# Retention decay factors: exponents built on VectorE in place of ScalarE's scale and bias

## The reference

```python
def retention_chunked(q, k, v, s0, log_gamma):
    diff = pos[:, None] - pos[None, :]
    decay = jnp.exp(jnp.where(diff >= 0, diff * lg, -jnp.inf))
...
        scores = jnp.einsum('bhid,bhjd->bhij', qc, kc) * decay
        o = jnp.einsum('bhij,bhje->bhie', scores, vc) + jnp.einsum('bhid,bhde->bhie', qc * q_dec, s)
...
def bidir_prefix(scan_f, scan_b, lat_f, lat_b, ctx_f, ctx_b):
    o_cf, s_f = scan_f(*ctx_f, s0)
    o_cb, s_b = scan_b(*flip(ctx_b), s0)
    o_lf, _ = scan_f(*lat_f, s_f)
    o_lb, _ = scan_b(*flip(lat_b), s_b)
    return o_lf + o_lb[:, :, ::-1], o_cf + o_cb[:, :, ::-1]
```

## Time and profile before

| | |
|---|---|
| median of 3 runs | 2225.99 us (2222.12 to 2227.66) |
| the profiled execution | 2222.12 us, span 2220.3 us |
| mean granted TensorE clock | 0.952 |
| PE / DVE / ACT / POOL busy | 92% / 43% / 34% / 33% of the span |
| the retention stage | from 811 to 891 us of the span |

### The profile page before, as it was taken

One profiled execution on the slowest core, in us unless ns is written; L12 is line 12 of the kernel. 1 busy time (PEld: TensorE's weight loads), 2 busy tenths in 40 slices (PEclk: granted clock), 3 DMA queues, 4 the chain that ended last, 5 costly groups with the idle time before them and its releaser, 6 DMA issues.

```text
span 2220.3 us, 26492 instructions
## 1 busy us (share of the span) xinstructions
PE 2039.9 (92%) x9550; PEld 1691.7 (76%) x9550; DVE 944.2 (43%) x1397; ACT 749.8 (34%) x1051; POOL 732.3 (33%) x324
## 2 busy tenths in 40 slices
PE   5999999999899989689899999979588888999997
PEld 2999999999868764556788888757464756888886
DVE  5652476145436026973411111377836535121124
ACT  4221122112263144342432222445446343232331
POOL 0323233323224220332344443523330222543432
PEclk9999999999999999678999999989789998999999
DMA  7432344334222210001233232322130211322321
GB/s 310 133 113 76 114 142 145 101 114 146 71 67 77 66 55 20 10 1 57 76 101 107 91 101 92 113 67 76 53 113 8 68 58 57 114 90 91 114 81 61
DMA packets 53273, 197.19 MB, mean 89 GB/s; under 512 B 6304, under 2 KB 6864, under 8 KB 51408
## 3 DMA queue, kind: packets, MB, share of 16 engines
q1 hardware_dynamic: 44272, 162.98, 23.0%
q10 hardware_dynamic: 8928, 33.23, 4.3%
HBM read 194.09 MB, written 2.10 MB: 88 GB/s over the span
## 4 chain that ended last, share of the span: by engine, by line
PE 78%; issue 9%; DVE 6%; ACT 3%; POOL 2%; DMA 1%; SPq 0%; DVEq 0%; POOLq 0%; ACTq 0%; PEldq 0%
PE ps L1606 64%; PE ps L1620 2%; POOL wlo L497 2%; PE ps L1593 1%; PE ps L1594 1%; PE ps L1595 1%; PE ps L1864 1%; DMA ada_f<-ada_p 1%; PE ps L1799 1%; PE ps L1925 1%; PE ps L1792 1%; PE ps L1951 1%; DVE prod L1083 1%; DVE s_gla L1347 1%; PE ps L1840 1%
## 5 line engine op out<-in xcount | busy, mean ns | idle before, releaser
L497 POOL TENSOR_TENSOR wlo<-raw,whi 128x1024 fp32r<-128x1024 f32 x280 | 690.8, 2479 | 1370.8 <-ACT whi L533 1348.7
L1606 PE MATMUL ps<-h_hi,whi 128*128 128x512 f32 (+2 forms) x1584 | 515.4, 364 | 13.8 <-POOL wlo L497 6.6
L1606 PE MATMUL ps<-h_hi,wlo 128*128 128x512 f32 (+2 forms) x1584 | 512.8, 362 | 0.0
L1606 PE MATMUL ps<-h_lo,whi 128*128 128x512 f32 (+2 forms) x1584 | 512.4, 362 | 0.0
L533 ACT ACTIVATE whi<-raw 128x1024 fp32r<-128x1024 f32 x280 | 289.6, 1053 | 425.6 <-PE ps L1606 342.1
L1606 PEld LDWEIGHTS ps<-h_hi,whi 128*128 128x128 f32 x1584 | 290.4, 188 | 56.6 <-issue 10.8
L1606 PEld LDWEIGHTS ps<-h_lo,whi 128*128 128x128 f32 x1584 | 290.3, 189 | 33.6 <-issue 0.7
L1606 PEld LDWEIGHTS ps<-h_hi,wlo 128*128 128x128 f32 x1584 | 290.1, 188 | 33.5
L1606 PE MATMUL ps<-g_hi,wlo 128*128 128x512 f32 (+1 forms) x784 | 257.4, 364 | 0.0
L1606 PE MATMUL ps<-g_hi,whi 128*128 128x512 f32 (+1 forms) x784 | 257.4, 364 | 0.0
L1606 PE MATMUL ps<-g_lo,whi 128*128 128x512 f32 (+1 forms) x784 | 257.3, 364 | 0.0
(11 more groups left out here) (351 smaller groups left out, 2293.7 us busy)
## 6 DMA issues: line engine op xcount, KB each, us to landing
raw<-panels SPq DMA_DIRECT2D x280, 512.0 KB, 3.5
ada_w<-ada_t ACTq DMA_DIRECT2D x54, 512.0 KB, 4.2
ada_f<-ada_p SPq DMA_DIRECT2D x8, 1024.0 KB, 18.4
x_lat<-x_t SPq DMA_DIRECT2D x1, 2048.0 KB, 7.5
out<-x_lat SPq DMA_DIRECT2D x8, 256.0 KB, 2.2
x_ctx<-ctx_t SPq DMA_DIRECT2D x1, 1024.0 KB, 9.5
cond_b<-cond SPq DMA_DIRECT2D x1, 1024.0 KB, 23.0
ada_x<-ada_t SPq DMA_DIRECT2D x2, 512.0 KB, 21.3
```

The costliest lines, as they stand in the source:

```text
L497: pool.tensor_tensor(wlo[:, sl], raw[:, sl], whi[:, sl].bitcast(f32), ALU.subtract).then_inc(lo_done, 1)
L1606: ins = pe.matmul(bank(banks + b, n), wt[:, w], a[:, at_(kc, c0):at_(kc, c0) + n], start=kc == 0 and j == 0, stop=kc == n_k - 1 and j == 2)
```

## The change

The exponents are now built by DVE, and ACT only applies Exp, in place, without scale or bias.

- DVE gets `exponents(j)`: four tensor_scalar instructions from `u_sb`, two of 896 and two of 640 columns. For latent keys u is first clipped at 0 from below (forward) or above (backward). It signals `arg_ready`. It stands in DVE's queue directly ahead of `decays_of(j)`.
- ACT gets `exponentials(j)`: it waits for `arg_ready` and runs two Exp over the whole 1536 columns of `decay_f` and `decay_b`. It replaces both `backward_decays` and `forward_decays`, at the place of the latter, behind `head_out`.
- DVE's `decays_of(j)` masks each direction's latent part by the sign of u (two scalar_tensor_tensor of 896 columns, two SBUF inputs each) and then adds the two tables over all 1536 columns. Before it was a minimum of 896, an addition of 128 and an addition of 640.
- The waits for `u_loaded`, `lsig_ready` and the panel of the entry before move from ACT to DVE. Two small vectors, `lsig_ctx` and `nlsig_ctx`, and the two instructions that made them go away; so does the semaphore `decay_made`.

```diff
                     if n == WIN_CONTEXT:
-                        act.wait_ge(u_loaded, 16)
-                        act.wait_ge(lsig_ready, 1)
-                        act.wait_ge(panel_done, done(P_WIN + WIN[WIN_CONTEXT - 1][1]))
-                        backward_decays(0)
-                        forward_decays(0)
-
-            def backward_decays(j):
-                if j:
-                    act.wait_ge(decay_made, j)
-                act.activation(decay_b[:, 0:UW], u_sb[:, :], ACT.Exp, scale=nlsig[:, j:j + 1])
-                act.activation(decay_b[:, UW:], u_sb[:, 256:], ACT.Exp, bias=nlsig_ctx[:, j:j + 1], scale=nlsig[:, j:j + 1])
-
-            def forward_decays(j):
-                if j:
-                    act.wait_ge(s_evac, 6 * j)
-                act.activation(decay_f[:, 0:UW], u_sb[:, :], ACT.Exp, scale=lsig[:, j:j + 1])
-                act.activation(decay_f[:, UW:], u_sb[:, 256:], ACT.Exp, bias=lsig_ctx[:, j:j + 1], scale=lsig[:, j:j + 1]).then_inc(exp_ready, 1)
+                        exponentials(0)
+
+            def exponentials(j):
+                act.wait_ge(arg_ready, j + 1)
+                act.activation(decay_f[:, :], decay_f[:, :], ACT.Exp)
+                act.activation(decay_b[:, :], decay_b[:, :], ACT.Exp).then_inc(exp_ready, 1)
 
             def retention():
                 for j in range(HEADS):
-                    if j + 1 < HEADS:
-                        backward_decays(j + 1)
                     head_out(j)
                     if j + 1 < HEADS:
-                        forward_decays(j + 1)
+                        exponentials(j + 1)
...
             def retention():
+                dve.wait_ge(u_loaded, 16)
+                dve.wait_ge(lsig_ready, 1)
+                dve.wait_ge(panel_done, done(P_WIN + WIN[WIN_CONTEXT - 1][1]))
+
+                def exponents(j):
+
+                    lg_f, nlg_b = lsig[:, j:j + 1], nlsig[:, j:j + 1]
+                    if j:
+                        dve.wait_ge(s_evac, 6 * j)
+                    dve.tensor_scalar(decay_f[:, 0:UW], u_sb[:, :], 0.0, lg_f, ALU.max, ALU.mult)
+                    dve.tensor_scalar(decay_b[:, 0:UW], u_sb[:, :], 0.0, nlg_b, ALU.min, ALU.mult)
+                    dve.tensor_scalar(decay_f[:, UW:], u_sb[:, 256:], float(CTX), lg_f, ALU.add, ALU.mult)
+                    dve.tensor_scalar(decay_b[:, UW:], u_sb[:, 256:], -float(LAT), nlg_b, ALU.add, ALU.mult).then_inc(arg_ready, 1)
+
                 def decays_of(j):
                     dve.wait_ge(exp_ready, j + 1)
-                    link(dve.tensor_tensor(decay_f[:, 0:UW], decay_f[:, 0:UW], decay_b[:, 0:UW], ALU.min))
-                    dve.tensor_tensor(decay_f[:, 384:384 + P], decay_f[:, 384:384 + P], ident[:, :], ALU.add)
-                    dve.tensor_tensor(decay_f[:, UW:], decay_f[:, UW:], decay_b[:, UW:], ALU.add).then_inc(decay_made, 1)
-                    dve.wait_ge(decay_made, j + 1)
-
+                    dve.scalar_tensor_tensor(decay_f[:, 0:UW], u_sb[:, :], 0.0, decay_f[:, 0:UW], ALU.is_ge, ALU.mult)
+                    link(dve.scalar_tensor_tensor(decay_b[:, 0:UW], u_sb[:, :], 0.0, decay_b[:, 0:UW], ALU.is_le, ALU.mult))
+                    link(dve.tensor_tensor(decay_f[:, :], decay_f[:, :], decay_b[:, :], ALU.add))
+
+                exponents(0)
                 decays_of(0)
...
                     if j + 1 < HEADS:
+                        exponents(j + 1)
                         decays_of(j + 1)
```

More of the change, by code:

```diff
@@ L201, in build @@
         lsig = at("lsig", 16, R_VEC + 1568)
-        nlsig_both = at("nlsig_both", 8, R_VEC + 1632)
-        nlsig, lsig_ctx = nlsig_both[:, 0:4], nlsig_both[:, 4:8]
+        nlsig = at("nlsig", 4, R_VEC + 1632)
         ls_tmp = at("ls_tmp", 4 * 16, R_TMP + 11 * KB + 512)
@@ L217, in build @@
         cs2 = at("cs2", 2 * LAT, R_TMP + 8 * KB)
-        rope_decay = at("rope_decay", 6, R_VEC + 1376)
-        rope_pp, nlsig_ctx = rope_decay[:, 0:2], rope_decay[:, 2:6]
+        rope_pp = at("rope_pp", 2, R_VEC + 1376)
         bias_sb = at("bias_sb", LT * LAT, R_ADA)
@@ L274, in build @@
             sem(n) for n in ("win_evac", "rope_loaded", "rope_done", "u_loaded", "masks_loaded"))
-        decay_made, exp_ready, s_ready, s_evac, pv_done = (sem(n) for n in ("decay_made", "exp_ready", "s_ready", "s_evac", "pv_done"))
+        arg_ready, exp_ready, s_ready, s_evac, pv_done = (sem(n) for n in ("arg_ready", "exp_ready", "s_ready", "s_evac", "pv_done"))
         o_ready, o_copied, mean_ready, o_centred, osq_ready, var_ready, oroot_ready, o_scaled, ohi_done, mix_ready = (
@@ L1179, in log_sigmoids @@
                 link(dve.scalar_tensor_tensor(lsig[:, :], lsig[:, :], 0.0, p, ALU.min, ALU.subtract))
-                link(dve.tensor_scalar(nlsig[:, :], lsig[:, 4:8], -1.0, None, ALU.mult))
-                dve.tensor_scalar(lsig_ctx[:, :], lsig[:, 0:4], float(CTX), None, ALU.mult)
-                dve.tensor_scalar(nlsig_ctx[:, :], nlsig[:, :], -float(LAT), None, ALU.mult).then_inc(lsig_ready, 1)
+                dve.tensor_scalar(nlsig[:, :], lsig[:, 4:8], -1.0, None, ALU.mult).then_inc(lsig_ready, 1)
             def residual(p0, o0, gate, m):
```

## The result

The kernel after takes 2243.37 us (median of 5 runs, 2238.64 to 2247.63), the kernel before, timed beside it, 2225.99 (5 runs, 2222.12 to 2227.66). The ratio is 1.0082, with a 95% interval of 1.0060 to 1.0102: slower, and within 1.6 us of the forecast of 2245 (the prediction's own sum, 2226.0 + 19.5, gives 2245.5, by which it is 2.1). The profiled execution of the kernel after took 2242.82, its span 2241.0 at a mean granted clock of 0.947; before it was 2222.12, 2220.3 and 0.952. One of the eleven executions of a later kernel (the mean inside the filler, without early rounding) took 2385.36 us at a granted clock of 0.822 and is left out of that kernel's ratio, though not of its median.

What follows compares the result with a forecast made beforehand. PE, busy 92% of the span, bounds the kernel; its waits in the retention stage decide. Delays of 1.2, 3.3, 4.2 and 4.2 (12.9) plus 6.6 of clock make 19.5 on 2226.0: 2245 us, range 2235 to 2253.

Steps and rivals of the forecast that it cites:

- The bound and the slack: Retention stage: PE sets the pace; DVE's table work has 0.17 us slack before centring at heads three and four.
- ACT's Exps: Behind `head_out`: two Exps of 1.49 us, 2.87 together; table load of 1.28 exposed ahead of heads three and four.
- e: End of ACT's last Exp; forecast -0.7 us at head one, +1.35 at two, +2.45 at three and four.
- DVE's exponents, hidden: Ahead of heads three and four: four DVE instructions, 2.1 us, ready at 844.5 before the table load ends at 845.0.
- DVE's masks: In `decays_of`: each mask of 896 columns costs 1.09 us, at full rate rather than half.
- The hold: All four boundaries: POOL's subtraction holds DVE instructions with two SBUF inputs; table work ends at e + 6.28, +1.94 us.
- The clock: Behind PE's idles of 4.0 us once and 4.9 twice: clock falls to 0.50, costing 2.2 us three times, 6.6.
- Around the stage: Outside the stage from 811 to 891: nothing gets longer; the stage alone grows by 17 to 22 us.
- No hold: Rival: POOL's subtraction does not hold DVE's masks; 2.3 us less per boundary, +3.8, 2230 us; chance 0.06.
- The clock stays up: Rival: PE's idles do not lower the clock; only the 12.9 us of delays, 2239 us; chance 0.10.
- The clock stays low for the first half of each head: Rival: 3.0 us per slow stretch, 1.5 ahead of the first head; +23.4, 2249 us; chance 0.09.
- Off the path: Rival: decays could be made early enough to hide; judged forbidden by DVE's queue; no chance given.

Runs made afterwards that it cites:

- the mean inside the filler, without early rounding: Kernel before, with the mean moved into the middle of the filler and the square ahead of the filler's Silu, panel rounding left in place: 2223.99 us, ratio 0.9994.
- early rounding: ACT's rounding of filler panels moved to the head's start, so POOL subtracts there; on the kernel before: 2223.02 us, ratio 0.9985.
- the load hidden: Kernel after, plus an unused one-column Exp ahead of the second and third head's `head_out`: 2243.52 us, ratio 1.0078.
- the kernel with early rounding: Kernel after, with ACT's rounding of filler panels moved to the head's start, so POOL subtracts there: 2227.97 us, ratio 1.0014.
- the masks alone: Kernel before, with ACT's four Exps kept and only DVE's combining changed to two masks and one sum of 1536 columns: 2233.53 us, ratio 1.0040.
- PE kept busy: Kernel after, plus four spare matmuls into an unused bank ahead of the average of squares at three boundaries: 2235.16 us, ratio 1.0042.
- the last kernel: Kernel before, with early rounding, mean inside the filler, square and root ahead of Silu, and rounding ahead of the backward Exps: 2216.96 us, ratio 0.9960.

## Why the prediction was right

The time, the sign and the mechanism held, and each term came within 0.35 us of its size. By its own steps:

- **The bound and the slack.** Right. PE paces the stage, and the centring had so little slack that nearly all delay of the table reached PE. That early rounding gives the kernel before nothing behind the first head, and 2.1 us at it, confirms which boundaries the mean sets.
- **ACT's Exps.** Right: two of 1.49 and 1.47 against the predicted 1.49, e at 858.01, 4.78 behind the start of `head_out`, where it was 2.33: +2.45 as predicted. The load fell between the copy and the first Exp ahead of heads three and four, without a drain. "ScalarE: Activation LUTs" of the Trainium skill (What ACT_TABLE_LOAD costs) would add one; the trace shows 0.01 us between load and Exp.
- **DVE's exponents, hidden.** Right ahead of heads three and four. They end at 854.77 and the load at 855.13. Their cover is thin, 0.36: with the load gone the first Exp started 1.57 behind the copy instead of 1.91, and what it waited for were they.
- **DVE's masks.** Price right: 1.09 and 1.08 for 896 columns. The half rate of which the Trainium skill speaks ("Vector Engine (DVE) Microarchitecture Reference", Points that are easy to get wrong) was not seen in them.
- **The hold.** The mechanism is shown: with the subtraction elsewhere, the sum takes 1.76 instead of 3.79 and the addition of 128 columns 0.29 instead of 2.37. The mis-sized item is the order: I let POOL win at the second mask, with the work ending at e + 6.28. In the kernel after DVE won at all four boundaries and the work ended 5.94 behind e (858.01 to 863.95); the prediction's other branch gave e + 6.1. Of these 0.34 us the order makes 0.19 (6.10 against 5.91); of the rest, 0.07 is that the first mask starts 0.03 behind e and not 0.1, and 0.08 that in this order too the work took 6.10 and not 6.18. Over four boundaries that is 1.4, a little more than the distance between 12.9 and 11.8. The Trainium skill ("SBUF — State Buffer", Who interferes with whom) describes ports that DVE and GpSimd lock for a whole instruction, the first to issue winning and the other blocked; the trace agrees with both outcomes, 3.30 for POOL in one kernel and 3.29 for the mask in the other. Which of the two issued first it does not show: POOL's record starts first every time.
- **The clock.** The mechanism is right: keeping PE busy removed these three terms. That the sum fits, 6.7 us against 6.6, is partly luck. It came as 2.5 + 1.4 + 2.8 and not as 2.2 three times, and in the kernel with the load hidden, whose idles are nearly the same, it was 5.5, distributed in another way. The five timed runs of the kernel after span 9 us, the longest (2247.63) at the lowest mean clock, 0.942, and the shortest (2238.64) at the highest, 0.949.
- **Around the stage.** No change was predicted there. The 3.6 us ahead and the -1.4 behind make the two profiled executions differ by 2.2 more than their stages. The profile before was 3.9 under its median, the profile after only 0.55 under its own; so the medians differ by 18.5 + 2.2 - 3.3 = 17.4. That 17.4 lies near the predicted 19.5 is in that part luck: what lies outside the stage nearly cancels.

The rivals. *No hold* gave +3.8; the kernel with early rounding shows what that is like, +3.7 on the stage, but the kernel after is held. *The clock stays up* did not happen. *The clock stays low for the first half of each head* came true for two heads of three (6.8 us at 0.50, 2.5 and 2.8 us lost), and not for the third (3.4 us, 1.4 lost). *Off the path* did not happen.

Who wins the tie is not settled. POOL's record starts 0.01 to 0.02 us ahead of the second mask's wherever DVE won, at 13 boundaries of four kernels with these masks (the kernel after, the masks alone, PE kept busy, the load hidden). It starts 0.08 ahead at two of the three where POOL won, and 0.02 at the third, in the kernel with PE kept busy. Read to the nanosecond, that one lead is 21 ns and the thirteen are 9 to 19, so a threshold between them fits, but by 2 ns. For the two leads of 0.08 ACT's rounding ended 0.85 us behind the start of the first mask, at the others 0.91 to 0.93. I did not vary it by itself, and that chance plays no part is not shown.

What stays open: why the first head's idle of 3.25 or 3.26 us left the clock at 1.00 in two executions (the kernel after, the masks alone) and came with 0.50 in two others (PE kept busy, the load hidden), though up to there three of the four kernels run the same instructions in this stage, and why it survived 3.78 in one kernel and fell behind 2.88 in another.

## What to carry to other kernels

Moving work from an engine with time to spare (ACT) to another with time to spare (DVE) is not free when both stand in the same hop that PE waits for; what counts is the length of the hop, and not the busy shares. When a short DVE instruction shows a long time, look at what POOL does in the same microseconds, and move POOL's instruction before you shorten DVE's: here that was worth 14.8 us on the changed kernel, of whose 18.5 us over the kernel before only 3.7 were left. And a PE idle of about 4 us cost the idle and, in most cases here, 1.4 to 2.8 us of slow clock on top (once, at 3.78, nothing), so two small delays can cost more together than the sum of each alone.

## What the runs showed of the hardware

- The hold is mutual. POOL's subtraction took 3.30 us in place of 2.43 when a mask with two SBUF inputs was running.
- A one-source `tensor_scalar` took longer beside POOL too: ahead of the first head, L1277 took 1.41 us beside POOL's subtraction (timelines of DVE and POOL of the kernel after), and 0.69 ahead of the third head, where POOL was idle. It ended 0.49 behind the subtraction; in the four other kernels with these exponents it took 1.34 to 1.48 there and ended 0.47 or 0.48 behind.

```profile
805.41 1.41 DVE L1277 TENSOR_SCALAR decay_f<-u_sb,lsig 128x896 f32<-128x896 f32 x1 [89.67 <-DMA u_sb<-u_tab]
```
```profile
803.94 2.39 POOL L495 TENSOR_TENSOR wlo<-raw,whi 128x1024 fp32r<-128x1024 f32 x1 [6.09 <-ACT whi L531]
```

- The product of a PSUM tile with the table (`s_ring`) kept its 0.69 and the reciprocal of 128 columns its 0.94 beside POOL's 856.22 to 858.58 in the last kernel. That is what its order uses.
